# Joining the small matrix products of a chunked RWKV-7 scan over 128 partitions

## What is computed

```
def rwkv_step(S, inp):
    r, w, k, v, a, b = inp
    sa = jnp.einsum('bdhvk,bdhk->bdhv', S, a)
    S = S * w[..., None, :] + sa[..., None] * b[..., None, :] + v[..., None] * k[..., None, :]
    return S, jnp.einsum('bdhvk,bdhk->bdhv', S, r)
```

## Time and profile before

| | us |
|---|---|
| median of 3 runs (lowest, highest) | 2538.04 (2537.2, 2542.55) |
| the profiled execution | 2535.24 |
| its span | 2533.4 |
| scan stage, first POOL instruction to the last from_states (timeline) | 664.65 to 1023.8 |

### The profile page before, as it was taken

The page is one execution under the profiler, slowest core; times in us unless marked ns, Lnnn a source line. Parts: engine busy times, 40 slices in busy tenths (PEclk is TensorE's granted clock), DMA queues, the critical chain, the costliest instruction groups (busy, mean ns, idle before and its releaser), DMA issues.

```text
span 2533.4 us, 40846 instructions
## 1 busy us (share of the span) xinstructions
PE 2013.9 (79%) x16281; PEld 1230.6 (49%) x16281; DVE 1661.4 (66%) x3506; ACT 853.6 (34%) x1682; POOL 680.0 (27%) x577
## 2 busy tenths in 40 slices
PE   5999947888678788887899887777777777778877
PEld 3766635666667776575455432333333333333332
DVE  4699964687034344554776777777777777777764
ACT  4666633465434343223223222222222121212121
POOL 0000020000112121002344445444444444444441
PEclk8999978988689999898999999999989999988999
DMA  6477653523443231436999999999999999999995
GB/s 240 155 254 250 224 204 143 186 72 117 176 166 140 104 137 45 169 117 242 421 420 415 383 420 416 420 421 419 421 419 421 420 421 419 421 420 421 421 421 214
DMA packets 136029, 742.01 MB, mean 293 GB/s; under 512 B 17920, under 2 KB 25120, under 8 KB 69280
## 3 DMA queue, kind: packets, MB, share of 16 engines
q0 software_dynamic: 73728, 536.90, 51.1%
q1 hardware_dynamic: 60960, 200.41, 21.8%
q10 hardware_dynamic: 1152, 2.10, 0.2%
HBM read 683.67 MB, written 55.69 MB: 292 GB/s over the span
## 4 chain that ended last, share of the span: by engine, by line
DMA 30%; PE 15%; DVE 4%; issue 3%; ACT 2%; POOL 0%; DVEq 0%; ACTq 0%
DMA uv<-in_uv_in,ic 30%; PE bank L2654 13%; DVE junk L2539 2%; DMA scores_dram<-later 1%; PE bank L92 1%; PE bank L94 1%; PE bank L93 1%; ACT dg L2451 1%; PE bank L2635 1%; POOL uv L2374 0%; DVE wql L2503 0%; ACT ge L2446 0%; ACT L2446 0%; DVE gc_ L2544 0%; ACT L2291 0%
## 5 line engine op out<-in xcount | busy, mean ns | idle before, releaser
L2654 PE MATMUL bank<-uv,dg 128*128 128x512 f32 x1664 | 816.1, 648 | 212.2 <-ACT dg L2451 212.1
L2654 PEld LDWEIGHTS bank<-uv,dg 128*128 128x128 f32 x1664 | 335.4, 206 | 682.8 <-issue 404.3
L2374 POOL DMA_INDIRECT uv<-in_uv_in,ic x416 | 478.2, 1150 | 627.8 <-PE bank L2654 556.5
L2539 DVE SCALAR_TENSOR_TENSOR junk<-uv,gr 128x1024 f32<-128x1024 f32 x416 | 510.1, 1226 | 185.7 <-DMA uv<-in_uv_in,ic 158.1
L2446 ACT ACTIVATE ge<-dt_ 128x4 f32<-128x4 f32 (+1 forms) x130 | 26.7, 205 | 945.1 <-DVE junk L2539 945.0
L2654 PE MATMUL bank<-uvx,dg 128*128 128x512 f32 x384 | 185.7, 641 | 52.5 <-ACT dg L2451 52.5
L2451 ACT ACTIVATE dg<-ident,gc_ 128x128 f32<-128x128 f32 x512 | 163.9, 390 | 31.2 <-DVE gc_ L2544 29.1
L2539 DVE SCALAR_TENSOR_TENSOR junk<-uvx,gr 128x1024 f32<-128x1024 f32 x96 | 117.7, 1226 | 58.6 <-DMA uvx<-in_uv_in,ic 56.0
L2654 PEld LDWEIGHTS bank<-uvx,dg 128*128 128x128 f32 x384 | 76.4, 204 | 161.7 <-issue 90.1
L2374 POOL DMA_INDIRECT uvx<-in_uv_in,ic x96 | 114.5, 1193 | 120.8 <-PE bank L2654 110.4
L92 PE MATMUL bank<-hx_hi,wzh 128*128 128x512 f32 x160 | 70.5, 440 | 34.9 <-DVE wzl L984 19.4
(11 more groups left out here) (362 smaller groups left out, 3704.7 us busy)
## 6 DMA issues: line engine op xcount, KB each, us to landing
pair_record<-rec SPq DMA_DIRECT2D x32, 768.0 KB, 4.9
wt<-in_wrow_in SPq DMA_DIRECT2D x32, 512.0 KB, 4.4
wraw<-in_wpair_in SPq DMA_DIRECT2D x24, 512.0 KB, 3.6
xb<-pair_record SPq DMA_DIRECT2D x16, 768.0 KB, 6.2
wm<-in_wmod SPq DMA_DIRECT2D x4, 2048.0 KB, 20.9
wz<-in_wz_in SPq DMA_DIRECT2D x32, 256.0 KB, 3.3
wraw<-in_wq_in SPq DMA_DIRECT2D x16, 512.0 KB, 6.4
uv<-in_uv_in,ic POOLq DMA_INDIRECT x416, 28.1
```

Source lines behind the costliest of these rows:

```text
L2374: pool.indirect_dma_start(ring(i), None, g["uv_in"], bass.IndirectOffsetOnAxis(ap=ic[:, s % ICR, k:k + 1], axis=0)).then_inc(su[row_slot[i ...
L2539: dve.scalar_tensor_tensor(junk[:, :], ring(i)[:, 0:D], 1.0, hc[:, t % 2, :], ALU.mult, ALU.mult, accum_out=dt[:, k:k + 1]).then_inc(s_ud, 1)
L2654: mm = pe.matmul(acc(t, c)[:, :], dg[:, n % 2, k, :], ring(i)[:, D + 512 * c:D + 512 * c + 512], start=h == 0 and q == 0 and k == 0, stop= ...
```

## The change

k and b of a record are interleaved by chunk: k, b, b, k for the two chunks of a pair. One product has k and b of a chunk as 128 columns of weights and a and r together as 128 moving columns (line 1824 of the changed kernel); of its four blocks three are used. The quarter tiles of k and b are so arranged that the transposed k lies on the 64 partitions of its chunk and b on the other 64 (kr), and values and weights likewise (vp). So kt·vt + bt·pw is one product over 128 partitions, and so is rkb·vt + rkb·pw. The transition and gg, both with the carried removal (pa), become one product with 128 moving columns (carried) for the 8 latent chunks; the 4 context chunks keep one of 64 (transitions). All record fields that serve as moving operands lie in one tensor, var. lv and la now hold the decayed k and b (dkb) of the whole pair, so that both are loaded behind the last turn. The weighted copy of ACT becomes three, the masks of DVE are cut to 128 elements, and POOL's two products become four of half the size. The order in lines 1797 to 2028 of the changed kernel follows.

The diff, cut to its core; longer runs of removed lines stand in the kernel above:

```
-        ra, rk, rb = (rec[:, o:o + NDIR * T].rearrange("p (d c s) -> p d c s", d=NDIR, c=NC)
-                      for o in (RC_A, RC_K, RC_B))
+        ra = rec[:, RC_A:RC_K].rearrange("p (d c s) -> p d c s", d=NDIR, c=NC)
+        kb = rec[:, RC_K:RC_V].rearrange("p (d c w s) -> p d c w s", d=NDIR, c=NC // 2, w=4)
+        rk, rb = kb[:, :, :, 0:4:3, :], kb[:, :, :, 1:3, :]
+        pairs = lambda a: a.rearrange("p (c w s) -> p c w s", w=2, s=CHUNK)
...
+                        sp.wait_ge(s_k, 2 * j)
                         sp.wait_ge(s_b, 2 * j)
-                        stored("b", j - 1)
+                        stored("kb", j - 1)
...
+                    sp.dma_start(ab[:, j % 2, 0, :, :, :], record[j, :, RC_A:RC_K].rearrange(
+                        "p (d c s) -> p d c s", d=NDIR, c=NC)).then_inc(s_ab[j % 2], 16)
+                    sp.dma_start(ab[:, j % 2, 1, :, :, :].rearrange("p d (c w) s -> p (d c) (w s)", w=2), record[j, :, RC_K:RC_V].rearrange(
+                        "p (e w s) -> p e (w s)", w=4, s=CHUNK)[:, :, CHUNK:3 * CHUNK]).then_inc(s_ab[j % 2], 16)
...
+        kb = sb(st, "lkb", [P, NDIR, NC // 2, 4, CHUNK])
+        var = sb(st, "lvar", [P, 4, NDIR, NC, CHUNK])
+        lv, la = var[:, 0, :, :, :], var[:, 1, :, :, :]
+        lr = (var[:, 2, :, CC:NC, :], var[:, 3, :, CC:NC, :])
+        dkb = var[:, 0:2, :, :, :].rearrange("p q d c s -> p (q d c s)").rearrange("p (d c w s) -> p d c w s", d=NDIR, c=NC // 2, w=4)
...
+        kr = sb(st, "kbt_rkb", [P, NE, 2, 2, 2, CHUNK])
+        vp = sb(st, "vt_pw", [P, NE, 2, 2, CHUNK])
         ra = sb(st, "rhs_a", [P, NE, 2, 2, CHUNK])
-        pw = sb(st, "pw", [P, NE, 2, 2, CHUNK])
+        pa = sb(st, "pw_a", [P, NE, 2, CHUNK])
...
+                            sp.wait_ge(s_t, 12 * j)
+                        sp.dma_start(lv, field(j, RC_V)).then_inc(s_lv, 16)
...
+                    for d in range(NDIR):
+                        if d:
+                            pool.wait_ge(s_t, 12 * j + 6)
+                            pool.wait_ge(s_a, 2 * NR * j + 2 * NR)
+                        else:
+                            pool.wait_ge(s_t, 12 * j + 3)
+                        wide = e[:, d, :].rearrange("p (c w) -> p c w", w=2).unsqueeze(3).broadcast_to((P, NC // 2, 2, CHUNK))
+                        for w in (slice(0, 4, 3), slice(1, 3)):
+                            pool.tensor_tensor(dkb[:, d, :, w, :], kb[:, d, :, w, :], wide, ALU.mult).then_inc((s_kp, s_bp)[d], 1)
...
                     act.wait_ge(s_pw, 6 * j + r + 1)
-                    act.activation(pw[:, 2 * r:2 * r + 2, :, :, :], bank[2 + r % 3][:, :].rearrange(
-                        "p (e h q k) -> p e h q k", e=2, h=2, q=2), ACT.Copy).then_inc(s_pwc, 1)
+                    src = bank[2 + r % 3][:, :].rearrange("p (e h q k) -> p e h q k", e=2, h=2, q=2)
+                    for p in range(2):
+                        act.activation(vp[HALF[1 - p], 2 * r:2 * r + 2, p, :, :], src[HALF[1 - p], :, :, 0, :], ACT.Copy).then_inc(s_pwc, 1)
+                    act.activation(pa[:, 2 * r:2 * r + 2, :, :], src[:, :, :, 1, :], ACT.Copy).then_inc(s_pwc, 1)
...
+                    for h in range(2):
+                        dve.wait_ge(s_a, 2 * NR * j + 2 * n + h + 1)
+                        if n == 0:
+                            m = NE - NL
+                            dve.tensor_tensor(ka[:, 0:m, h, :], bank[h][:, 0:CHUNK * m].rearrange("p (e t) -> p e t", e=m),
                                               mgt[:, :].unsqueeze(1).broadcast_to((P, m, CHUNK)), ALU.mult).then_inc(s_am, 1)
...
+                            continue
+                        e = NE - NL + 2 * n - 2
+                        src = bank[h][:, :].rearrange("p (d c q t) -> p d c q t", d=2, c=2, q=2)
+                        for p in range(2):
+                            dve.tensor_tensor(ka[HALF[p], e:e + 2, h, :], src[HALF[p], :, p, 0, :],
+                                              mgt[HALF[p], :].unsqueeze(1).broadcast_to((64, 2, CHUNK)), ALU.mult).then_inc(s_am, 1)
+                        for d in range(NDIR):
+                            b = src[:, d, :, 1, :]
+                            dve.tensor_tensor(kr[:, e + d, :, h, 1, :], b[:, :, ::-1] if d else b,
+                                              (mge, mgr)[d][:, :].unsqueeze(1).broadcast_to((P, 2, CHUNK)), ALU.mult).then_inc(s_am, 1)
...
+                    for r in range(2):
+                        c0 = CC + 4 * r
                         for p in range(2):
...
+                    cp = CC // 2 + n - 1
+                    for d in range(NDIR):
+                        for p in range(2):
+                            for h in range(2):
+                                o = P * (2 * d + p)
+                                mm = pe.matmul(bank[h][:, o:o + P], kb[HALF[h], d, cp, 2 * p:2 * p + 2, :].rearrange("p q s -> p (q s)"),
+                                               var[HALF[h], 1:3 + j % 2:1 + j % 2, d, 2 * cp + p, :], start=True, stop=True)
+                                if d == 1 and p == 1:
+                                    mm.then_inc(s_a, 1)
...
                 def updates(j, r):
                     c0, n = ((0, 4), (4, 2))[r]
-                    pe.wait_ge(s_pwc, 6 * j + (5, 6)[r])
                     if r:
+                        pe.wait_ge(s_pwc, 18 * j + 18)
                         pe.wait_ge(s_nc, 4 * j + 2)
                     else:
+                        pe.wait_ge(s_pwc, 18 * j + 12)
                         pe.wait_ge(s_kvc, 3 * j + 3)
                     for x in range(2 * n):
                         e = 2 * c0 + x
-                        for lhs, rhs, q in ((kt, vt[:, e, :, :], 0), (bt, pw[:, e, :, 0, :], 1)):
+                        for p in range(2):
                             for h in range(2):
...
+                                mm = pe.matmul(bank[p][HALF[h], HEAD * x:HEAD * x + HEAD], kr[:, e, p, h, 0, :], vp[:, e, p, h, :],
+                                               start=True, stop=True)
+                            if x == 2 * n - 1:
+                                mm.then_inc(s_n, 1)
+
+                def transitions(j):
+                    for x in range(CC):
                         for h in range(2):
                             for p in range(2):
-                                mm = pe.matmul(bank[2 + p][HALF[h], HEAD * x:HEAD * x + HEAD], pw[HALF[p], e, h, 1, :],
-                                               bt[HALF[p], e, h, :], start=True, stop=True)
-                                if x == 2 * n - 1 and h == 1:
+                                mm = pe.matmul(bank[(2, 5)[p]][HALF[h], HEAD * x:HEAD * x + HEAD], pa[HALF[1 - p], x, h, :],
+                                               kr[HALF[1 - p], x, p, h, 0, :], start=True, stop=True)
+                                if x == CC - 1 and h == 1:
                                     mm.then_inc(s_m, 1)
 
-                def carried(j):
-                    pe.wait_ge(s_nc, 4 * j + 4)
-                    for x in range(NL):
+                def carried(j, r):
+                    if r:
+                        pe.wait_ge(s_mc, 6 * j + 3)
+                        pe.wait_ge(s_gc, 8 * j + 2)
+                    else:
+                        pe.wait_ge(s_pwc, 18 * j + 18)
+                    for x in range(4):
+                        e = NE - NL + 4 * r + x
                         for h in range(2):
                             for p in range(2):
...
+                                mm = pe.matmul(bank[MG[r][p]][HALF[h], P * x:P * x + P], pa[HALF[1 - p], e, h, :],
+                                               kr[HALF[1 - p], e, p, h, :, :].rearrange("p q k -> p (q k)"), start=True, stop=True)
+                                if x == 3 and h == 1:
+                                    mm.then_inc(s_m, 1)
...
                         pe.wait_ge(s_ys, j)
                     for cp in range(XC // 2):
                         for h in range(2):
...
+                            for d in range(NDIR):
+                                for p in range(2):
+                                    e, r = (2 * cp, p) if d == 0 else (2 * (XC // 2 - 1 - cp) + 1, 1 - p)
+                                    e += NE - NL
+                                    o = P * cp + HEAD * h
+                                    pe.matmul(bank[6 + r][HALF[p], o:o + HEAD], kr[:, e, r, h, 1, :], vp[:, e, r, h, :],
+                                              start=cp == 0 and h == 0, stop=False, skip_group_check=True)
 
...
+                            if c <= NR:
                                 products(j + 1, c - 1)
-                            if c == 1:
-                                turn(j + 1, 0)
-                            elif c < 5:
+                            if c < 7:
                                 turn(j + 1, c - 1)
-                            elif c < 9:
-                                turn(j + 1, 2 * c - 6)
```

(4 more changed lines are left out.)

## The result

The changed kernel took 2559.14 us (median of 9 runs), the kernel before 2537.2 us on the same chip. The ratio is 1.0088, its 95% interval 1.0072 to 1.0103: slower by 22 us, where 10 us faster was forecast. The profiled execution took 2557.22 us, its span 2555.4 (before 2533.4).

A forecast was written before the change was run, and what follows sets the result against it. Instruction-fetch stops of TensorE were taken to bound the scan's dense parts. Dense parts -38.5, chains +19.0, scan's start +5.5, last store +1.9, inversion +1.5 gave -10.6 us: 2527 us forecast, range 2508 to 2552.

The forecast's parts named there:

- The dense part: Scan, own to outputs: eight parts 159.9 us in sum instead of 198.38, a gain of 38.5 us.
- the waits left: Dense part: TensorE's remaining stops, 1.8 us a part instead of some 5.9, bounds 0 and 3.5.
- The reading as instruction fetch: Dense part: TensorE's stops are waits for blocks of 256 instructions, each taking about 3.7 us to come, longer under data transfers.
- The chain: Scan's ten steps between dense parts: 19.85 us instead of 17.14, 2.7 more each, 19.0 us lost over seven.
- eight masks take 7 x 0.20 + 0.29 = 1.69: Chain, DVE: masks of 128 elements start 0.20 us apart, making a product-and-mask round 2.83 us and four 11.3.
- third rival: Chain's mask rounds: a mask costs its full 0.29 us or TensorE gets 1.2 GHz; round 3.5, total 2550 us, chance 0.13.
- second rival: Dense part: the stops are not instruction fetch and stay at 5.9 us a pair; total 2558 us, chance 0.07.
- Lowered 0.6: Chain, after the masks end at 13.9 us: the step called lowered takes 0.6 us before step 6.
- The edges: Outside dense parts and chains: scan's start +5.5 us, projection's last store +1.9, inversion's reads of bonus keys +1.5.
- The stages ahead: Before the scan: 1.9 us for the projection's larger last store and 1.5 for the inversion's shorter reads.
- The bound of 10: Scan's start: upper bound of the 5.5 us loss, lower bound 3, as the clock can fall to 1.2 GHz.
- The range: Whole kernel: 2508 to 2552 us, taking in the third rival and leaving out the second and fourth.

The follow-up runs named there:

- e4: Changed kernel with 144 matmuls of 8 columns added in each pair's dense part, each ahead of a real one that overwrites it; 2639.89 us, ratio 1.0397.
- e11: Changed kernel with the receptance products' masks on all 128 partitions instead of 64, leaving one operand wrong, for timing only; 2529.07 us, ratio 0.9959.
- e13: Changed kernel with a round's eight masks reordered, the two on partitions 64 to 127 together at the end; 2555.16 us, ratio 1.0063.
- e2: Changed kernel with the low part of the previous pair's output (o_lo) taken after step 9 instead of step 5; 2542.29 us, ratio 1.0004.
- e12: Changed kernel with idle transposes of the unit matrix filling TensorE's waits at the scan's start and in step 6 of each chain; 2547.24 us, ratio 1.0046.
- e3: Changed kernel with PSUM banks 0 and 1 as one array, four masks of 256 elements a round instead of eight of 128; 2551.46 us, ratio 1.004.

## Why the prediction was wrong

**The dense part: right.** 159.9 us was predicted, 160.69 came; the waits left were put at 14 us or so and are 18.8. That the sum is so close is partly luck: the six usual parts took 20.6 us each instead of 20.0, the first 19.6 instead of 21.5 and the last 17.55 instead of 18.4. The reading as instruction fetch fits everything measured: the instruction queue brought 45 packets from 690 to 1036 us instead of 66, again one for 256 instructions; fewer instructions, less idle time; fewer bytes beside it, less idle time; other work fits into the waits. What it does not have is a run that changes the count alone, since e4's matmuls were work too.

**The chain: the failed step.** It is the line "eight masks take 7 x 0.20 + 0.29 = 1.69". They take 2.16 (769.97 to 772.13). The 0.20 came from operations that all began at partition 0; four of the eight masks are followed by one that begins at another partition, and that costs 0.11 to 0.12 each (e11, e13). With the product's 1.19 to its first mask instead of 1.09, a round is 3.41 instead of 2.83, 2.3 us a chain. The step was the disputed one: the third rival named the half partitions and a round of 3.5 us, the nearest to what happened, but got 0.13, and its time, 2550, was 9 us short. The second rival's 2558 is nearer to 2559.14 by accident: it had the stops for issue stay, and they fell from 47.8 to 18.8 us. Its ground, that a mask costs its full duration, holds for four of the eight masks (0.31 or 0.32 for one of 0.29), and for these because of the start partition; its other ground, a TensorE at 1.2 GHz, was met at the scan's start and behind the long wait, not in the chains' rounds.

**What followed from it.** "Lowered 0.6": 1.54 us, as the later masks put it beside GpSimd's product, 0.9 more; e2 and e11 bring back 0.68. The clock: behind TensorE's longer wait before step 7 it is halved for the transposes and a step, 1.5 us a chain. With the 2.3 of the rounds that is 4.7, where a usual chain (24.46) is 4.6 over 19.85. With the masks' spacing as predicted, and nothing else changed, the kernel took 2529.07 us (e11), against 2527 forecast. That this is so near is partly luck too: the scan itself, from its first instruction to the end of the last dense part, took 333.4 us in e11's profile, where the prediction's terms make 329.2 of the 343.2 before.

**The edges.** +5.5 was predicted for the scan's start, +9.4 came. The first product is 1.3 us later, where 2 were counted; from it to the first own it is 8.1 us more (25.98 instead of 17.87), where 3.5 were counted. The masks of four rounds are 1.9 of that, and most of the rest is the clock at 0.50, of which e12 brought back 3.4. The bound of 10 held it. The stages ahead took 4.7 instead of 3.4; over all profiles the scan starts at 664.65 to 667.2 us in the kernel before and its two variants, at 667.4 to 674.3 in the twelve with joined records, 4.4 later in the mean, so one profile can't tell the two numbers apart.

**The range** ended at 2552, 2 us above the third rival's own time, with no room for what a longer round brings with it.

**A version that beats both** is e1: joined operands in the dense part, products apart. 2501.23 us.

## What to carry to other kernels

Price an added operation with its neighbours: by a row with the same start partitions in the same order, not only the same size and engine. When a change joins parts that can be had separately, look for the one that gains and the one that pays; here undoing the products alone turned +22 us into -39. Here fewer, larger matmuls paid in the part where TensorE stood waiting for issue, and cost in the part where each must be emptied before the next.

## What the runs showed of the hardware

- A DVE operation that begins at partition 64 behind one that begins at 0, or the reverse, starts 0.30 to 0.32 us after it, where 0.20 is usual for 128 elements (e13), and 0.45 instead of 0.34 for 256 (e3). The Trainium skill, "VectorE: DVE Perf Modes", section "Two Vector instructions with no wait between them", states it: an operation whose input or output starts in another group of 32 partitions than the last one's is held until all earlier ones have finished. The trace agrees; the prediction did not use it.
- `o_lo`, with two inputs in SBUF, took 0.68 us alone. Behind a GpSimd product that had started first it took 1.54 (changed kernel), 1.79 (e13) or 1.93 us (e3), and each time it ended 0.55 us after that product did. GpSimd's own second product then took 1.92 us instead of 1.47:

```profile
781.81 1.47 POOL L1610 TENSOR_TENSOR lvar<-lkb,ec 128x768 f32<-128x768 f32 x1 [4.80 <-PE bank L1853]
783.24 1.92 POOL L1610 TENSOR_TENSOR lvar<-lkb,ec 128x768 f32<-128x768 f32 x1
```

  Where `o_lo` started first, by 0.01 us (e11), it took 0.68, and the GpSimd product beside it 2.00. So the later of the two waits for the earlier. The masks and sums, which read PSUM, kept their 0.28 to 0.29 beside GpSimd. The Trainium skill, "SBUF — State Buffer", section "Who interferes with whom", has the rule, that a DVE operation with two SBUF inputs and a GpSimd one that reads SBUF exclude each other; the trace agrees.
- A matmul record of 8 columns with its own weights costs 0.024 us, the mean over the 288 that e4 adds to a part, where one of 64 columns takes 0.029 two at a time.
- A wait of TensorE can be paid twice: its clock was 0.50 (1.2 of 2.4 GHz) in the two us that began 2 us after a wait of 2.36, and 1.00 there where transposes of no use filled the wait (e12).
